# Attention scores of a hybrid decoder layer as three fp32r products of split queries and keys, with another cut of the fourth query projection

## What is computed

```python
xp = _half_ffn(xp, ffn1...)                       # x + 1/2 SwiGLU(RMSNorm(x))
u, q, k, v = _project(_rmsnorm(xp), pos_p, w_in[l], q_norm[l], k_norm[l])   # 8 query heads, 2 key heads, 64 wide
mixed = concat([_pool_mix(u, ...), _swa_prompt(q, k, v, attn_sinks[l])])
xp = xp + mixed @ w_out[l]
xp = _half_ffn(xp, ffn2...)

def _swa_prompt(q, k, v, sinks):                  # blocks of 128 queries against 256 keys
    s = jnp.einsum('bnqhgd,bnkhd->bnhgqk', qb, k_band) * SCALE
    p = _sink_probs(s, mask, sink)                # softmax with a learned sink per head
    o = jnp.einsum('bnhgqk,bnkhd->bnqhgd', p, v_band)
```

## Time and profile before

| | us |
|---|---|
| median of 3 runs | 880.23 |
| lowest and highest | 879.8, 883.03 |
| the profiled execution | 880.45 |
| its span (first to last instruction) | 878.4 |
| PE busy | 871.3 |
| DVE busy | 660.3 |
| ACT busy | 394.0 |
| POOL busy | 32.4 |

### The profile page before, as it was taken

One profiled execution on the slowest core, in us unless ns is written; L12 is line 12 of the kernel. 1 busy time (PEld: TensorE's weight loads), 2 busy tenths in 40 slices (PEclk: granted clock), 3 DMA queues, 4 the chain that ended last, 5 costly groups with the idle time before them and its releaser, 6 DMA issues.

```text
span 878.4 us, 17072 instructions
## 1 busy us (share of the span) xinstructions
PE 871.3 (99%) x7088; PEld 856.9 (98%) x7088; DVE 660.3 (75%) x979; ACT 394.0 (45%) x639; POOL 32.4 (4%) x37
## 2 busy tenths in 40 slices
PE   8999999999999999999999999999999999999998
PEld 7999999999999999999888999999999999999998
DVE  6979647997569986754887697996479975799754
ACT  7635313554224553443754465554125542255420
POOL 0000000000000000012423000000000000000000
PEclk9999999999999999999999999999999999999999
DMA  7333323332424322522321415324233324334241
GB/s 251 117 121 114 133 66 121 121 121 84 145 65 164 121 76 84 190 76 60 113 65 60 145 38 169 120 76 175 75 121 120 121 85 145 111 122 128 85 121 61
DMA packets 43180, 98.57 MB, mean 112 GB/s; under 512 B 4288, under 2 KB 5056, under 8 KB 43104
## 3 DMA queue, kind: packets, MB, share of 16 engines
q1 hardware_dynamic: 41376, 95.01, 33.6%
q10 hardware_dynamic: 1728, 2.48, 0.8%
HBM read 93.53 MB, written 3.60 MB: 111 GB/s over the span
## 4 chain that ended last, share of the span: by engine, by line
PE 96%; DVE 2%; DMA 1%; issue 1%; ACT 0%; SPq 0%; DVEq 0%; ACTq 0%
PE ps L612 44%; PE ps L740 15%; PE ps L742 15%; PE ps L741 15%; PE ps L642 1%; PE ps L978 1%; PE ps L969 1%; DMA xT<-x 1%; PE ps L960 1%; PE ps L799 1%; PE ps L933 0%; PE ps L883 0%; PE ps L657 0%; DVE wlo L1522 0%; DVE hlo L1649 0%
## 5 line engine op out<-in xcount | busy, mean ns | idle before, releaser
L740 PE MATMUL ps<-xhi,whi 128*128 128x260 f32 (+1 forms) x1092 | 310.2, 284 | 0.1
L742 PE MATMUL ps<-xhi,wlo 128*128 128x260 f32 (+1 forms) x1092 | 310.0, 284 | 0.0
L741 PE MATMUL ps<-xlo,whi 128*128 128x260 f32 (+1 forms) x1092 | 309.6, 284 | 0.0
L740 PEld LDWEIGHTS ps<-xhi,whi 128*128 128x128 f32 x1092 | 205.4, 188 | 0.8 <-issue 0.6
L742 PEld LDWEIGHTS ps<-xhi,wlo 128*128 128x128 f32 x1092 | 205.5, 188 | 0.0
L741 PEld LDWEIGHTS ps<-xlo,whi 128*128 128x128 f32 x1092 | 205.4, 188 | 0.0
L1593 DVE TENSOR_TENSOR wlo<-full,whi 128x1024 fp32r<-128x1024 f32 (+1 forms) x117 | 160.3, 1394 | 0.0
L1118 ACT CAST whi<-raw 128x1024 fp32r<-128x1024 f32 (+1 forms) x75 | 75.2, 1003 | 154.9 <-PE ps L612 147.9
L612 PE MATMUL ps<-hhi,whi 128*128 128x268 f32 (+1 forms) x690 | 140.4, 285 | 0.3
L612 PE MATMUL ps<-hlo,whi 128*128 128x268 f32 (+1 forms) x690 | 140.1, 284 | 0.0
L612 PE MATMUL ps<-hhi,wlo 128*128 128x268 f32 (+1 forms) x690 | 139.8, 284 | 0.0
(11 more groups left out here) (194 smaller groups left out, 1070.4 us busy)
## 6 DMA issues: line engine op xcount, KB each, us to landing
full<-gu SPq DMA_DIRECT2D x78, 512.0 KB, 4.4
raw<-d SPq DMA_DIRECT2D x32, 448.0 KB, 3.5
full<-gu SPq DMA_DIRECT2D x39, 256.0 KB, 2.7
raw<-d SPq DMA_DIRECT2D x16, 512.0 KB, 3.7
raw<-w_in SPq DMA_DIRECT2D x10, 512.0 KB, 3.7
raw<-gu SPq DMA_DIRECT2D x9, 512.0 KB, 4.3
raw<-w_out SPq DMA_DIRECT2D x8, 512.0 KB, 4.3
xT<-x SPq DMA_DIRECT2D x8, 268.0 KB, 5.8
```

The source lines that it names most:

```text
L740: nc.tensor.matmul(dst, whi_t, xhi_t, start=(first and pr == 0), stop=False, skip_group_check=True)
L741: nc.tensor.matmul(dst, whi_t, xlo_t, start=False, stop=False, skip_group_check=True)
L742: last = nc.tensor.matmul(dst, wlo_t, xhi_t, start=False, stop=(pr == KC - 1), skip_group_check=True)
```

## The change

1. **Scores.** `qT` and `kT` give way to split tiles: `qhi` (in its place), `qlo` (four tiles, one for each query projection), `khi`, `klo`. Each score is now the sum of three fp32r products, hi x hi, `qlo` x `khi`, `qhi` x `klo`; in a step 12 products stand where 4 were, and the two heads of a pair alternate. `scores(0)` waits for `klo` and the first two `qlo`, `scores(4)` for the other two.
2. **Who makes the parts.** ACT casts `khi` from `kT` and `qhi` from `hid` (`q_hi(1)` to `q_hi(4)`, in its row at four places), DVE subtracts `klo` and `qlo` of the first two, POOL `qlo` of the last two.
3. **POOL.** The sum of a query now stays in `hid`, so the product of the next query, which overwrites `hid`, waits until `qlo` has been taken. The decode queries are copied to `dq` after each query, two copies of 8 columns, not at the end.
4. **PE's order.** `project(5)` runs six of its eight chunks ahead of scores(0) instead of four, and `project(6)` six ahead of turn_probs(0) and two behind `q_sums(3)`, instead of four and four.

The diff, cut to its core:

```diff
-        project(5, half[0])
+        project(5, [0, 1, 2, 3, 4, 5])
@@ scores
             if i == 0:
-                pe.wait_ge(rot_ready, 3)
+                pe.wait_ge(klo_ready, 1)
+                pe.wait_ge(qlo_ready[0], 1)
+                pe.wait_ge(qlo_ready[1], 1)
                 pe.wait_ge(root_ready, 4)
...
             elif i == 4:
-                pe.wait_ge(rot_ready, 5)
+                pe.wait_ge(qlo_ready[2], 1)
+                pe.wait_ge(qlo_ready[3], 1)
...
-            for k in (0, 2, 1, 3):
-                g, j = head_of(i, k)
-                rows = slice(g * HD, (g + 1) * HD)
-                last = nc.tensor.matmul(dst[k], qT[rows, j, t * P:(t + 1) * P], kT[rows, t * P:(t + 2) * P],
-                                        start=True, stop=True)
-                if j % 2:
-                    last.then_inc(scored, 1)
+            queries, keys = slice(t * P, (t + 1) * P), slice(t * P, (t + 2) * P)
+            for pair_of_heads in ((0, 2), (1, 3)):
+                for part in range(3):
+                    for k in pair_of_heads:
+                        g, j = head_of(i, k)
+                        rows = slice(g * HD, (g + 1) * HD)
+                        q = qlo[j][rows, queries] if part == 1 else qhi[rows, j, queries]
+                        last = nc.tensor.matmul(dst[k], q, (klo if part == 2 else khi)[rows, keys],
+                                                start=(part == 0), stop=(part == 2))
+                        if part == 2 and j % 2:
+                            last.then_inc(scored, 1)
@@ after scores(0), scores(1)
-        project(5, half[1])
-        project(6, half[0])
+        project(5, [6, 7])
+        project(6, [0, 1, 2, 3, 4, 5])
@@ after q_sums(3)
-        project(6, half[1])
+        project(6, [6, 7])
@@ ACT
+        def q_hi(x):
+
+            act.wait_ge(rot_ready, x + 1)
+            nc.scalar.copy(qhi[:, x - 1, :], hid[:, META:NT]).then_inc(qhi_ready, 1)
@@ DVE
+        def q_lo(x):
+
+            dve.wait_ge(qhi_ready, x)
+            nc.vector.tensor_tensor(qlo[x - 1][:, :], hid[:, META:NT], qhi[:, x - 1, :].bitcast(F32), ALU.subtract
+                                    ).then_inc(qlo_ready[x - 1], 1)
...
+        q_lo(1)
         rotate(2)
+        dve.wait_ge(khi_ready, 1)
+        nc.vector.tensor_tensor(klo[:, :], kT[:, :], khi[:, :].bitcast(F32), ALU.subtract).then_inc(klo_ready, 1)
...
         take_z(3)
+        q_lo(2)
         split_next(4)
@@ POOL
             if x == 1:
                 pool.wait_ge(qk_ready, 1)
+            elif x:
+                pool.wait_ge(qlo_ready[x - 2], 1)
             nc.gpsimd.tensor_tensor(hid[:, cols], zg[:, x % 2, cols], cosT[:, cols], ALU.mult
                                     ).then_inc(cos_ready, 1)
...
-            dst = hid[:, :] if x == 0 else qT[:, x - 1, :]
-            nc.gpsimd.tensor_tensor(dst, hid[:, cols], sq[:, cols], ALU.add).then_inc(rot_ready, 1)
+            nc.gpsimd.tensor_tensor(hid[:, cols], hid[:, cols], sq[:, cols], ALU.add).then_inc(rot_ready, 1)
...
+            for g in range(KVH) if x else ():
+                rows = slice(g * HD, (g + 1) * HD)
+                nc.gpsimd.tensor_copy(dq[rows, :, g, x - 1], hid[rows, TP:NT]).then_inc(dq_ready, 1)
+            if x:
+                pool.wait_ge(dq_ready, KVH * x)
+            if x > 2:
+                pool.wait_ge(qhi_ready, x)
+                nc.gpsimd.tensor_tensor(qlo[x - 1][:, :], hid[:, META:NT], qhi[:, x - 1, :].bitcast(F32), ALU.subtract
+                                        ).then_inc(qlo_ready[x - 1], 1)
```

More of the change, by code:

```diff
@@ L201, in build @@
     prob, prob_end = place("prob", [P, 2, GQ, 2 * P], offset=upn_at)
-    assert prob_end <= t4_end
+    qlo0, o = place("qlo0", [P, NOUT], F32R, offset=prob_end)
+    assert o <= t4_end
     sq, _ = place("sq", [P, NT])
+    sqsum_at = at[0]
     sqsum, _ = place("sqsum", [P, NT])
+    qlo1, _ = place("qlo1", [P, NOUT], F32R, offset=sqsum_at)
     fixed, _ = place("fixed", [P, N_FIXED])
@@ L236, in build @@
     assert o <= xlo_at
-    qT, o = place("qT", [P, GQ, NOUT], offset=xlo_end)
+    qlo2, _ = place("qlo2", [P, NOUT], F32R, offset=xhi_end + NT * 4)
+    qhi, o = place("qhi", [P, GQ, NOUT], F32R, offset=xlo_end)
+    qlo3, _ = place("qlo3", [P, NOUT], F32R, offset=o)
+    qlo = [qlo0, qlo1, qlo2, qlo3]
     cosT, o = place("cosT", [P, NT], offset=o)
@@ L264, in build @@
     dscore, o = place("dscore", [HD, P], offset=o)
+    khi, o = place("khi", [P, PAD + NT], F32R, offset=o)
+    klo, o = place("klo", [P, PAD + NT], F32R, offset=o)
     assert o <= raw_at
@@ L337, in build @@
     dq_ready = sem("dq_ready")
+    khi_ready = sem("khi_ready")
+    klo_ready = sem("klo_ready")
+    qhi_ready = sem("qhi_ready")
+    qlo_ready = [sem(f"qlo_ready{x}") for x in range(1, 5)]
     dscores_filled = sem("dscores_filled")
@@ L986, in decode_scores @@
             pe.wait_ge(newk_placed, 1)
-            pe.wait_ge(dq_ready, KVH)
+            pe.wait_ge(dq_ready, KVH * GQ)
             pe.wait_ge(probT_ready, 2)
@@ L1409, in _ @@
         spread_z(2)
+        act.wait_ge(pads_zero, 1)
+        act.wait_ge(qk_ready, 1)
+        nc.scalar.copy(khi[:, :], kT[:, :]).then_inc(khi_ready, 1)
         def q_root(r):
@@ L1415, in q_root @@
             return nc.scalar.activation(qnrm[:, 0, cols], nsum[:, r, cols], ACT.Sqrt, scale=1.0, bias=eps64[:, 0:1])
+        q_hi(1)
         q_root(0).then_inc(root_ready, 1)
@@ L1420, in _ @@
         split_next(4)
+        q_hi(2)
         spread_z(3)
@@ L1423, in _ @@
         exps(1)
+        q_hi(3)
         spread_z(4)
@@ L1435, in _ @@
         split_next(6)
+        q_hi(4)
         out_hi(1)
@@ L2110, in _ @@
             pool.wait_ge(sin_ready, x + 1)
-            dst = hid[:, :] if x == 0 else qT[:, x - 1, :]
-            nc.gpsimd.tensor_tensor(dst, hid[:, cols], sq[:, cols], ALU.add).then_inc(rot_ready, 1)
+            nc.gpsimd.tensor_tensor(hid[:, cols], hid[:, cols], sq[:, cols], ALU.add).then_inc(rot_ready, 1)
             pool.wait_ge(rot_ready, x + 1)
-        pool.wait_ge(pads_zero, 6)
-        for g in range(KVH):
-            rows = slice(g * HD, (g + 1) * HD)
-            nc.gpsimd.tensor_copy(dq[rows, :, g, :], qT[rows, :, SEQ:NOUT].rearrange("p j b -> p b j")
-                                  ).then_inc(dq_ready, 1)
-            pool.wait_ge(dq_ready, g + 1)
+            if x == 1:
+                pool.wait_ge(pads_zero, 6)
+            for g in range(KVH) if x else ():
[7 more added lines that the diff above has]
+                                        ).then_inc(qlo_ready[x - 1], 1)
         def pool_lo(g):
```

## The result

The changed kernel takes 884.77 us (median of 22 runs, 883.1 to 886.61), the kernel before 882.11 in the same comparison (22 runs, 879.8 to 883.49). The ratio is 1.003 (95% interval 1.0021 to 1.0039): slower by 2.66 us, within the 0.5% that counts as no change. The forecast was +2.1 and 882.5, with a range of 879.7 to 884.9; the measured time lies 0.1 under the upper end of the range.

A forecast was written before the change was run, and what follows sets the result against it. TensorE, busy 99% of the span, was taken as the bound, so only waits or work reaching it count. 0.8 (way to attend(0)) + 1.6 (window sums) - 0.3 (scores) = +2.1 on 880.45 gave 882.5 us, range 879.7 to 884.9.

The forecast's parts named there:

- The scores: PE's scores steps: a pair of fp32r products takes 0.12, a step 0.14 less; only steps 5 and 7 count, -0.3 us.
- the second rival: Slower: half-row fp32r products not side by side or not in one pass, pair 0.24, step 1.65; 884.5 to 885.5, chance 0.14.
- Six chunks: PE runs two more projection chunks ahead of scores(0), putting it at 415.1; up to attend(0) a delay of 1.5 is free.
- First part: Way to attend(0): casts, subtractions and POOL/DVE collisions delay it 2.3, 1.5 of it work done early: +0.8; +0.1 without collisions.
- Second part: POOL's window sums, moved behind q_lo(4), meet DVE operations three times at 0.9, delaying take_u(1) and pool_map(0): +1.6, bounds 0 to 3.3.
- the forecast's own mechanism: Two to four meetings of DVE with the window sums, collisions or none ahead of attend(0): 881.4 to 884.2, chance 0.60.
- The first (meetings cost nothing): DVE and POOL operations slip past one another, or casts and copies are quicker: -0.2, 880.2 us, chance 0.20.
- The third (faster): Neither delay costs anything and all eight scores steps give their 0.14: -1.1, 879.3 us, chance 0.06.

The follow-up runs named there:

- the experiment with two buffers: Changed kernel with rotated queries written in turn to two buffers, `act_gate` for q1 and q3, `hid` for q2 and q4: 884.23 us, ratio to before 1.0026.
- the run with the sums first: Changed kernel with POOL's window_sums(0) ahead of q_lo(4) instead of behind it: 882.21 us, ratio to before 1.0002.
- the versions with every piece moved: Changed kernel with two query buffers and q_hi(3), window_sums(0), q_lo(3), q_lo(4) moved: 881.36 us; also one projection chunk ahead of attend(0): 880.87; three chunks: 880.70.

## Why the prediction was right

**The scores: right.** The step of two is 0.12 x 12 + 0.21 from 414.92 on, a pair 0.12 as taken, the second rival's 0.24 did not come. That steps 5 and 7 alone count was right as well: steps 3, 4 and 6 each end in a wait of 0.20 for `probT`.

**Six chunks: right.** scores(0) came at 414.92 where 415.1 was said, with no wait, and the cut alone costs nothing. With the old cut, 0.99 is waited for q_lo(2).

**First part: the events as forecast, 0.5 instead of 0.8, the cause only in part.** POOL's cos product of q2 began at 409.12 (409.2 said) after waiting for q_lo(1); rotate(2) was stretched to 1.37; rotate(3) came at 418.93 (419.2) and attend(0) at 426.48 (426.9). But the experiment with two buffers shows that the wait of the cos product was not the cause of the collision: without it the cos product meets q_lo(1). The lower end of this term, +0.1 if nothing collided, was not reached by taking away that wait. What the casts and subtractions ahead of attend(0) cost without any collision was not measured by itself.

**Second part: right in mechanism, 1.9 instead of 1.6.** The sums began at 437.61, not 436.5, because the half clock had pushed turn_probs(1) back and q_hi(4) with it. They were met three times, as taken, at 0.8, 0.9 and 1.1. The fourth meeting, 0.7, was with q_lo(4), which the sum had left out. Of the 3.5 us they cost DVE, 1.9 reached PE. pool_map(0) waited for take_u(1), as said, at 449.89 (448.4).

**What was missing: the half clock.** The sum held waits and work only. In the profiled execution each of the two longer waits is followed by a half-clock stretch that cost 1.6 and 1.5 in that execution. Over all runs it is worth 2.66 less 1.8 to 2.0, some 0.8, since the kernel before has such stretches as well in three runs out of four. The median of three runs ahead of the prediction (880.23) happened to be that of the runs at 1.0, and the same sum from the median of all would have come out at 884.2. So the account of the waits was right, and that the time itself still lies in the range is partly luck: it is over the 881.4 to 884.2 of the forecast's own mechanism, in the part of the range that was put there for the second rival.

**Rivals.** The first (meetings cost nothing) fell with the four stretched operations, and the run with the sums first shows their price. The second gave 884.5 to 885.5, and the measured time lies in that; its pair of 0.24 and its step of 1.65 are not in the trace. The third (faster) fell with the first: seen from the kernel before, even the versions with every piece moved don't show a gain.

## What to carry to other kernels

A wait of about a microsecond ahead of TensorE can be paid twice, once as idle time and once more as half clock behind it; so compare runs at the same granted clock first, and try work in the wait, though here it took the half clock out of some executions only. Where DVE and GpSimd both work on SBUF, moving one operation out of a collision can put its neighbour into it, as it did twice here: count all operations of the stretch with two SBUF inputs, not the one that was stretched. Splitting an fp32 product into three fp32r ones saves little where the copy behind it, and not the product, sets the step.

## What the runs showed of the hardware that was not expected

**Order between the halves of the rows.** Two products on different halves run side by side even where three others of one half stand between them in the program: the upper half's first one started at the lower half's first, ahead of two that precede it. With six ahead it started beside the third (424.49 against 424.14, 0.35 later), ahead of the three behind that. So two products were passed over in one trace and three in the other. The Trainium skill (TensorE: Matmul & The Clock Gate, Part 3) says that products are never reordered; the starts in these two traces don't agree with that, where the halves of the rows differ.

**Half clock behind short idle times and short products.** In the changed kernel the granted clock fell behind PE's waits of 0.62 and 1.18 followed by q_sums (products of 2 columns), and behind one of 1.82. A wait is neither needed nor enough. In the kernel before with a chunk moved it fell behind q_sums with no wait listed, as shown above. In the kernel with the scores head by head, pool_map(0) waited as long, and ran at full clock (1.15):

```profile
449.90 1.15 PE L945 MATMUL ps<-gate,poolw 128*128 128x260 f32 x4 [1.83 <-DVE up L1866]
```

In the kernel with only the cut moved it fell without a wait, behind decode_attend's 16 products of 8 columns (PE's windows: stretch, busy, granted clock, DMA share, GB/s):

```profile
452.00:457.50 5.50, 5.46 (x46) 1.00 0.32 100
457.50:461.00 3.50, 3.50 (x18) 0.52 0.00 0
```

Why it falls in some executions of the same kernel and not in others stays open.
